# The end of a decoder layer: where the first sums of the last expert, the row statistics and the second token tile's scaling are done

## The reference

```python
hm = x * (1 + sc2) + sh2
# best expert group of 4, the top 2 experts in it, 16 experts in all
for e in range(N_EXPERTS):
    hid = jax.nn.silu(t @ w_gate[e]) * (t @ w_up[e])
    y = y + combine[:, e:e + 1] * (hid @ w_down[e])
x = layer_norm(DEEPNORM_ALPHA * x + g2 * f, ln2_g[l], ln2_b[l])
...
# layer_norm: (x - mean) * rsqrt(var + 1e-5) * g + b, over the 2048 columns of a token
```

## Time and profile before

| what | us |
|---|---|
| median of 3 executions | 1790.05 |
| lowest and highest | 1787.77, 1793.58 |
| the profiled execution | 1788.96 |
| its span from first to last instruction | 1787.1 |
| TensorE busy in it | 1689.7 |
| VectorE busy | 601.3 |
| ScalarE busy | 186.5 |
| last weights landed, from the span's start | 1756.2 |
| last store issued, from the span's start | 1783.4 |

### The profile page before, as it was taken

The page is one execution under the profiler, slowest core; times in us unless marked ns, Lnnn a source line. Parts: engine busy times, 40 slices in busy tenths (PEclk is TensorE's granted clock), DMA queues, the critical chain, the costliest instruction groups (busy, mean ns, idle before and its releaser), DMA issues.

```text
span 1787.1 us, 22339 instructions
## 1 busy us (share of the span) xinstructions
PE 1689.7 (95%) x9444; PEld 992.1 (56%) x9444; DVE 601.3 (34%) x1080; ACT 186.5 (10%) x440; POOL 361.4 (20%) x161
## 2 busy tenths in 40 slices
PE   7799999999999999989899999899999989899986
PEld 6578888888888878643344443333434224334322
DVE  0453657877667143331120311112111111111114
ACT  0001013110011100140100010100101001001001
POOL 0005730277777768200000000000000000000000
PEclk9899999999999999989999999999999999999998
DMA  9997895678877564359958899999999999899995
GB/s 385 423 427 209 352 399 229 277 316 348 341 312 326 244 267 176 123 237 429 424 246 349 361 402 426 426 386 426 424 427 427 427 428 427 367 425 424 428 427 205
DMA packets 51028, 630.10 MB, mean 353 GB/s; under 512 B 5775, under 2 KB 8240, under 8 KB 11848
## 3 DMA queue, kind: packets, MB, share of 16 engines
q1 hardware_dynamic: 49768, 623.15, 84.0%
q10 hardware_dynamic: 1120, 5.01, 0.7%
HBM read 624.47 MB, written 3.67 MB: 351 GB/s over the span
## 4 chain that ended last, share of the span: by engine, by line
PE 74%; DMA 18%; DVE 4%; issue 1%; POOL 1%; SPq 0%; ACT 0%; DVEq 0%; POOLq 0%; ACTq 0%
PE bank L1415 23%; PE bank L865 22%; PE bank L877 10%; PE bank L1177 8%; DMA ring<-in_w_up_gate 7%; DMA ring<-in_ada_w 4%; PE bank L836 3%; DMA region_g<-in_w_up_gate 3%; PE bank L889 3%; PE bank L1253 2%; DMA region_g<-in_w_down 2%; DMA ring<-in_w_down 2%; DVE ada_rows L1944 2%; DMA ring<-in_w_in 1%; POOL ring L736 1%
## 5 line engine op out<-in xcount | busy, mean ns | idle before, releaser
L865 PE MATMUL bank<-ring,region_b 128*64 128x512 f32 x1792 | 407.3, 603 | 33.2 <-DMA ring<-in_w_up_gate 31.3
L736 POOL TENSOR_TENSOR ring<-ring 128x1024 f32<-128x1024 f32 x152 | 359.0, 2389 | 331.5 <-DMA ring<-in_w_in 224.6
L865 PEld LDWEIGHTS bank<-ring,region_b 128*64 128x64 f32 x1792 | 124.5, 138 | 287.6 <-issue 253.3
L877 PE MATMUL bank<-ring,region_f 128*64 128x512 f32 (+1 forms) x1312 | 225.6, 528 | 6.7 <-DMA ring<-in_w_down 6.7
L1415 PE MATMUL bank<-ring,region_a 128*128 128x256 f32 x768 | 171.3, 380 | 0.5 <-ACT region_g L1739 0.5
L1415 PE MATMUL bank<-ring,region_x 128*128 128x256 f32 x768 | 170.4, 379 | 0.9 <-issue 0.7
L1415 PEld LDWEIGHTS bank<-ring,region_a 128*128 128x128 f32 x768 | 145.3, 190 | 23.0 <-issue 2.7
L1415 PEld LDWEIGHTS bank<-ring,region_x 128*128 128x128 f32 x768 | 145.3, 190 | 21.1 <-issue 1.1
L877 PEld LDWEIGHTS bank<-ring,region_f 128*64 128x64 f32 (+1 forms) x1312 | 74.4, 128 | 140.4 <-issue 117.9
L1944 DVE SCALAR_TENSOR_TENSOR bank<-ring,condT,bank 128x512 f32<-128x512 f32 x192 | 144.8, 754 | 5.8
L2378 DVE TENSOR_TENSOR region_a<-bank,region_a 128x512 f32<-128x512 f32 x128 | 79.7, 683 | 179.3 <-PE bank L889 179.0
(11 more groups left out here) (235 smaller groups left out, 1314.6 us busy)
## 6 DMA issues: line engine op xcount, KB each, us to landing
ring<-in_w_up_gate SPq DMA_DIRECT2D x112, 2048.0 KB, 19.3
ring<-in_w_down SPq DMA_DIRECT2D x56, 2048.0 KB, 16.1
ring<-in_ada_w SPq DMA_DIRECT2D x44, 2048.0 KB, 11.9
ring<-in_w_in SPq DMA_DIRECT2D x31, 2048.0 KB, 13.8
region_g<-in_w_up_gate SPq DMA_DIRECT2D x16, 2048.0 KB, 18.3
ring<-in_w_branch SPq DMA_DIRECT2D x8, 2048.0 KB, 14.5
ring<-in_w_out SPq DMA_DIRECT2D x8, 2048.0 KB, 9.9
region_g<-in_w_down SPq DMA_DIRECT2D x8, 2048.0 KB, 23.3
```

What stands on the lines that cost most here:

```text
L736: ins = pool.tensor_tensor(quarter(s, *out)[:, k:k + 4, :], quarter(s, *in0)[:, k:k + 4, :], quarter(s, *in1)[:, k:k + 4, :], op)
L865: last = nc.tensor.matmul(bank_of(x, j)[n * c:n * c + n, 0:2 * m], tokens(x, 8 * half + k), w[:, k % 4, :, m * c:m * c + m], start=(half = ...
L877: last = nc.tensor.matmul(bank_of(x, q)[n * c:n * c + n, 0:m], hidT[x][:, k, :], w[:, k % 4, m * c:m * c + m], start=(k == 0), stop=(k == ...
```

## The change

Four things are altered.

1. For every turn's last expert, `add_up(le, 0)` on TensorE stands ahead of the wait for the last weights, not behind it.
2. For the very last expert VectorE makes four of the eight `bn_stats`, those of columns 0 to 1023 of both tiles, directly behind its sums of output half 0 (`early_stats`), which is ahead of `scale(1)`. The other four, and both `bn_aggr`, follow the sums of output half 1.
3. Tile 1 gets the treatment of tile 0: its own diagonal matrix in `work`, beta by TensorE into the banks 6, 7, 2, 3, and for q = 0, 1, 2 the matmul by TensorE and the copy by ScalarE. Part 3 of tile 1 is centred on VectorE, and then scaled there with beta read from its bank.
4. For both tiles the diagonal matrix is made before the four centred parts, not behind them. SyncE's waits follow: seven stores wait for ScalarE, the last for VectorE.

```diff
--- before.py
+++ after.py
@@ -242,7 +242,8 @@
     return (2 * t + h) % TURN_HALVES % E_PLACES
 
 
-NORM_BANKS = (0, 1, 4, 5)
+NORM_BANKS = ((0, 1, 4, 5), SUM_BANKS)
+BY_PE = ((0, 1, 2, 3), (0, 1, 2))
 LAST_USE = [max(range(i, TURN_HALVES, E_PLACES)) for i in range(E_PLACES)]
 
 
@@ -347,7 +348,7 @@
         hidT = [region_f[:, a:a + 8 * n].rearrange("p (k s) -> p k s", s=n)
                 for a, n in ((0, 64), (512, 32), (768, 32), (1024, 64), (1536, 64))]
         ysb = [sgu_wT[:, 0:512], sgu_wT[:, 512:1024]]
-        row_scale = work[:, 0:P]
+        row_scale = [work[:, 0:P], work[:, P:2 * P]]
         silu_g = [work[:, 0:256], work[:, 256:512]]
         hid = [work2[:, 0:256], work2[:, 256:512]]
         hidx = [None, work[:, 512:640], work[:, 640:768], work[:, 768:1024], work2[:, 512:768]]
@@ -511,6 +512,7 @@
         centred_ready = sem("centred_part_ready")
         scale_ready = sem("diagonal_scale_ready")
         normed_full = sem("normed_part_full")
+        beta_full = sem("beta_of_last_part_full")
 
         block = ctx.enter_context(nc.Block())
 
@@ -717,7 +719,10 @@
             for a in range(TT):
                 for q in range(4):
                     cols = slice(q * 512, (q + 1) * 512)
-                    sp.wait_ge(out_ready if a else tile_out, q + 1)
+                    if q in BY_PE[a]:
+                        sp.wait_ge(tile_out, 4 * a + q + 1)
+                    else:
+                        sp.wait_ge(out_ready, 1)
                     sp.dma_start(out_d[a * P:(a + 1) * P, cols], acc[:, a, cols]).then_inc(s_out, 16)
             sp.wait_ge(s_out, 16 * 4 * TT)
 
@@ -1155,10 +1160,10 @@
             down(0, 1, first).then_inc(half_used, 1)
             if 0 < len(xs) < 3:
                 extra("add F")(1)
-            loaded_half(5, 1)
             early = le == GRP - 1 and not xs
             if early:
                 add_up(le, 0)
+            loaded_half(5, 1)
             down(0, 1, last).then_inc(y_full, 1)
             if len(xs) == 2:
                 extra("add F")(2)
@@ -1568,13 +1573,20 @@
             pe.wait_ge(s_ln2, 32)
             pe.wait_ge(y_ready, 2 * NE + 2)
             pe.wait_ge(t_taken, 3 * NE + 1)
-            for q in range(4):
-                mm(psum[NORM_BANKS[q]][:, :], ident, ln2b[:, q * 512:(q + 1) * 512], True, False)
-            pe.wait_ge(scale_ready, 1)
-            for q in range(4):
-                pe.wait_ge(centred_ready, q + 1)
-                mm(psum[NORM_BANKS[q]][:, :], row_scale, acc[:, 0, q * 512:(q + 1) * 512], False, True)\
-                  .then_inc(normed_full, 1)
+            pe.wait_ge(extras_added, NE)
+            for a in range(TT):
+                for q in range(4):
+                    if a == 1:
+                        pe.wait_ge(m_taken[q], add_job(NE // GRP - 1, GRP - 1, 1, True) + 2)
+                    ins = mm(psum[NORM_BANKS[a][q]][:, :], ident, ln2b[:, q * 512:(q + 1) * 512], True,
+                             q not in BY_PE[a])
+            ins.then_inc(beta_full, 1)
+            for a in range(TT):
+                pe.wait_ge(scale_ready, a + 1)
+                for q in BY_PE[a]:
+                    pe.wait_ge(centred_ready, 4 * a + q + 1)
+                    mm(psum[NORM_BANKS[a][q]][:, :], row_scale[a], acc[:, a, q * 512:(q + 1) * 512], False, True)\
+                      .then_inc(normed_full, 1)
             for g, le, count, here in asked:
                 more_tokens(pe, f"pe{g}_{le}", mybir.EngineType.PE, count, here,
                             lambda xs: expert_pe(pe, mm, g, le, xs))
@@ -1851,10 +1863,11 @@
                     asked.append((g, le, count, here))
             for a in range(TT):
                 root(TT, a)
-            for q in range(4):
-                act.wait_ge(normed_full, q + 1)
-                act.activation(acc[:, 0, q * 512:(q + 1) * 512], psum[NORM_BANKS[q]][:, :], ACT.Copy)\
-                   .then_inc(tile_out, 1)
+            for a in range(TT):
+                for q in BY_PE[a]:
+                    act.wait_ge(normed_full, 4 * a + q + 1)
+                    act.activation(acc[:, a, q * 512:(q + 1) * 512], psum[NORM_BANKS[a][q]][:, :], ACT.Copy)\
+                       .then_inc(tile_out, 1)
             for g, le, count, here in asked:
                 more_tokens(act, f"act{g}_{le}", mybir.EngineType.Activation, count, here,
                             lambda xs: expert_act(act, g, le, xs))
@@ -2393,6 +2406,15 @@
                                 dve.wait_ge(m_full[b], add_job(g, of, q, not more) + 1)
                                 add(psum[SUM_BANKS[b]], q, a, c).then_inc(m_taken[b], 1)
 
+                    def early_stats():
+
+                        if ne == NE - 1:
+                            for b in range(len(SUM_BANKS)):
+                                dve.wait_ge(m_taken[b], add_job(g, le, 0, not more) + 2)
+                            for a in range(TT):
+                                for q in range(2):
+                                    dve.bn_stats(lstat[:, a, q, :], acc[:, a, q * 512:(q + 1) * 512])
+
                     if xs:
                         extra("mark")(xs[0])
                     if xs and le > 0:
@@ -2413,10 +2435,12 @@
                     early = le == GRP - 1 and not xs
                     if early:
                         add_up(le, 0)
+                        early_stats()
                     scale(1)
                     if le == GRP - 1:
                         if not early:
                             add_up(le, 0)
+                            early_stats()
                         add_up(le, 1)
                         for b in range(len(SUM_BANKS)):
                             dve.wait_ge(m_taken[b], add_job(g, le, 1, not more) + 2)
@@ -2451,23 +2475,26 @@
             mark_tokens(0)
             rests = [turn_of_experts(g, g < NE // GRP - 1) for g in range(NE // GRP)]
 
-            dve.wait_ge(s_ln2, 32)
             for a in range(TT):
-                for q in range(4):
+                for q in range(2, 4):
                     ins = dve.bn_stats(lstat[:, a, q, :], acc[:, a, q * 512:(q + 1) * 512])
                 link(ins)
                 dve.bn_aggr(lmv[:, a, :], lstat[:, a, :, :].rearrange("p n s -> p (n s)")).then_inc(l_var, 1)
-                if a == 0:
-                    dve.wait_ge(l_var, TT + 1)
-                    for q in range(4):
-                        part = acc[:, 0, q * 512:(q + 1) * 512]
-                        dve.scalar_tensor_tensor(out=part, in0=part, scalar=lmv[:, 0, 0:1],
-                                                 in1=ln2g[:, q * 512:(q + 1) * 512], op0=ALU.subtract, op1=ALU.mult)\
-                           .then_inc(centred_ready, 1)
-                    dve.wait_ge(l_std, TT + 1)
-                    link(dve.reciprocal(lrstd[:, 0:1], lrstd[:, 0:1]))
-                    dve.tensor_scalar(row_scale, ident, lrstd[:, 0:1], None, ALU.mult).then_inc(scale_ready, 1)
-            scaled(acc, ln2g, ln2b, 1, TT, out_ready)
+            dve.wait_ge(s_ln2, 32)
+            for a in range(TT):
+                dve.wait_ge(l_var, TT + a + 1)
+                dve.wait_ge(l_std, TT + a + 1)
+                link(dve.reciprocal(lrstd[:, a:a + 1], lrstd[:, a:a + 1]))
+                dve.tensor_scalar(row_scale[a], ident, lrstd[:, a:a + 1], None, ALU.mult).then_inc(scale_ready, 1)
+                for q in range(4):
+                    part = acc[:, a, q * 512:(q + 1) * 512]
+                    dve.scalar_tensor_tensor(out=part, in0=part, scalar=lmv[:, a, 0:1], in1=ln2g[:, q * 512:(q + 1) * 512],
+                                             op0=ALU.subtract, op1=ALU.mult).then_inc(centred_ready, 1)
+            dve.wait_ge(beta_full, 1)
+            dve.wait_ge(centred_ready, 4 * TT)
+            last_part = acc[:, 1, 3 * 512:4 * 512]
+            dve.scalar_tensor_tensor(out=last_part, in0=last_part, scalar=lrstd[:, 1:2], in1=psum[NORM_BANKS[1][3]][:, :],
+                                     op0=ALU.mult, op1=ALU.add).then_inc(out_ready, 1)
             for rest in rests:
                 rest()
```

## The result

The changed kernel took 1791.12 us (median of 20 executions, 1786.86 to 1793.22), the kernel before 1787.78 us (20, 1785.26 to 1793.58). The ratio is 1.0017 (95% interval 1.0010 to 1.0023): 3 us slower, still within 0.3%. The forecast was 1784.9 us with a range up to 1788.2, so the time is outside it, on the wrong side of the kernel before.

What follows compares the result with a forecast made beforehand. The kernel's end was taken to be VectorE, then a queue of stores, then one landing. Issuing the eighth store 5.1 us earlier, with the same 3.71 us behind it, turned the median 1790.05 into 1784.9 us, range 1783.0 to 1788.2.

Steps and rivals of the forecast that it cites:

- the zero for everything ahead of the end: Everything before the kernel's end: costed at zero, as the order of TensorE's instructions stays.
- the moved waits of the first three turns: Last experts of the first three turns: moved weight waits costed at zero; up to 1.2 us gain each if weights were late.
- Step 1: Last expert: first sums run at 1755.0 ahead of the weight wait, so the last down half ends 1.2 us earlier.
- Step 2: VectorE at the end: early statistics delay `scale(1)`, leaving it and everything behind 0.50 us earlier, not 1.2; bad bound 0.06.
- Steps 3 and 4: Final tiles: VectorE's part ends at 1776.5; TensorE sets the end, 15 calls unbroken from 1764.0, seventh copy ending 1777.9.
- Step 5: Last stores: eighth issued at 1778.3, 5.1 us earlier, with the same 3.71 us behind it to the span's end at 1782.0.
- my estimate from the Trainium skill: Last store's landing: 2.6 us for 256 KB, which would make the sum about -5.8 us.
- the clock did not fall: Rival, chance 0.20: TensorE idles 1.5 us before the second sums, clock halves, its chain ends 1.7 us later; 1786.6 us.
- the slower rival: Rival, chance 0.04: TensorE at half clock for all 15 calls at the end; median 1797.4 us.
- The faster landing: Rival, chance 0.15: the last store lands in 2.6 us, 0.7 us off the forecast, giving 1784.2 us.
- The stores did queue: Rival, chance 0.12: spaced last stores still block each other at issue, cutting the gain to 3.7 us: 1786.3 us.

Runs made afterwards that it cites:

- with the jump put back: The whole change with 230 never-executed counter instructions added on TensorE, putting the jump back at place 233; 1783.44 us, ratio 0.9971 against the kernel before.
- The run with the split: The change with old code places, tile 1's two early statistics moved behind `scale(1)`; 1782.88 us, ratio 0.9977 against the kernel before.
- the five unchanged ends: Profiled executions of the kernel before, plain and with 20, 26, 46 and 86 never-executed increments; ending on average 35.35 us behind the last down unit's start.

## Why the prediction failed

**The step that failed** is in the first paragraph: "none of that is touched" and "So only the end counts". The order of TensorE's instructions upstream was untouched, as I had read from it, but not their places. By padding alone this is worth 7 us (4 to 9) in the kernel before, more than the whole gain: 4.7 to 4.9 us for one jump of TensorE, and 2.1 to 2.5 us for the half clock behind the wait. The term that failed is the zero for everything ahead of the end. Its stated reason held, for the moved waits of the first three turns cost nothing: with the jump put back the last down unit starts within 0.1 us of where it did. The list of what would be wrong had "an end elsewhere in the kernel than here, such as weights landing at another time than 1756 us", and this is what happened, but with no rival and no price. The price was in the trace: among the jumps of that trace one takes 7.25 us for no wait that the profile names. A rival "the longer program costs one such fetch" would have given up to +7 us behind a gain of 5, hence anything from the forecast to 2 us slower.

**Step 1, the first sums**: right. They begin 3.58 us behind the start and the last down half 1.3 us earlier than before.

**Step 2, the early statistics**: right. They end at 1766.50, `scale(1)` follows at once, and the second sums are 0.68 us earlier where 0.50 was forecast. TensorE's idle time there is 1.42 us, 1.5 in the forecast. The run with the split shows that 0.6 us of this was to be had.

**Steps 3 and 4**: right. VectorE's part never holds TensorE up, the eight beta calls and seven diagonal ones run from 1769.1 to 1782.2, and the copies come 0.86 us apart. That gives the 25.6 us of the forecast.

**Step 5**: the issue of the eighth store was right to 0.1 us, and the term behind it was mis-sized. I kept 3.71 us from issue to the span's end; it was 5.07 us after, 4.65 in the same kernel with its jump put back, and 4.1 to 5.2 in all the others, those with an unchanged end too. The row of 3.71 is the shortest of 14 profiled executions; the other four with this end have 4.2 to 5.0. The stores' line, with the time from issue to landing, in the kernel after:

```profile
L726 SPq DMA_DIRECT2D out<-region_a x8: 332/340/1044, 1777.7 to 1783.6; - x8
...
DMA to landing us min/median/max: 2.5/2.9/4.7
```

The median store does land in 2.9 us, near the 2.6 us of my estimate from the Trainium skill ("DMA: Bandwidth & Descriptors", "Anatomy of one DMA"). The slowest takes 4.7, and the span ends 5.07 us behind the last issue. By that rule the sum would be further from the measurement than by the row.

**The rivals.** At the end the clock did not fall; windows of the kernel after over TensorE's idle stretch, the beta calls and the diagonal ones (width, busy us of PE, PEld, DVE, ACT, POOL, granted clock, DMA share, GB/s):

```profile
1765.73:1767.15 1.42, 0.00 (x1) 0.00 (x0) 1.37 (x3) 0.00 (x0) 0.00 (x0) 1.00 0.00 0
1767.20:1776.00 8.80, 8.80 (x24) 3.79 (x25) 6.93 (x14) 0.59 (x2) 0.00 (x0) 1.00 0.00 0
1776.00:1782.20 6.20, 6.20 (x15) 2.47 (x13) 5.21 (x10) 3.59 (x6) 0.00 (x0) 1.00 0.51 181
```

An idle stretch of 1.42 us was followed by full clock, and with it falls the slower rival too. The fall that did come was upstream, behind the 5.56 us of the jump, where no rival had looked. The faster landing did not come where it counts: the median went from 3.3 us to 2.9, but the longest from 3.9 to 4.7. The stores did queue once: the sixth took 1.04 us to issue where five others took 0.34, which held up the seventh, ready at 1782.85, to 1783.10. That is 0.25 us, and the copy had been ready 0.3 us ahead of the forecast.

**The changed end against its forecast**, with the jump put back: 5.2 us faster by the ratio (3.2 to 7.0), 5.1 forecast. That they agree this closely is in part luck. The medians give 4.2 us, and the end itself is 4.3 us shorter than in the profiled execution before, 3.9 us shorter than the average of the five unchanged ends. The row that the sum started from was out of the common at both of its last terms: its eighth store went at 32.10 us where the other four unchanged ends have 30.4 to 31.1, and its landing of 3.71 us was the shortest. The two errors offset each other in the span.

## What to carry to other kernels

When an edit changes how many instructions an engine's program has, look at every jump to or from code that stands further on: an unrelated jump can move to the start of a fetch block, and then the whole engine waits, and may find its clock at half behind the wait. Sort the branch instructions of the trace by duration before and after, and if one has grown, pad with code that never runs (or move code) before judging the edit. Take the time behind the last store as a range from several executions, not as one row.

## What was not expected of the hardware

- A jump of TensorE to far code, announced ahead, takes 0.31 to 0.47 us; the jump of expert 2, 3 instructions into a block of 256, took 5.06 and 5.27 us, 23 instructions in 2.31, 63 in 0.33, and at places 233 and 253 0.34 to 0.35.
- Each long one of these ended 1.37 to 1.40 us behind the end of a 16 KB packet on the instruction queue q8.
- TensorE's granted clock was 1.00 before the 5.56 and 5.35 us of idleness and 0.50 for 5.1 and 4.3 us behind them; behind 2.60 us it stayed at 1.00.
- A jump that is not announced took 7.2 to 7.9 us for expert 2, the only one that takes it. The other two records of its line, 0.07 us each, are of experts that go on to the section that stands next. An announcement right behind another had no effect on it.
- Of eight stores of 256 KB the slowest landed 4.2 and 4.7 us behind its issue where the median was 2.9. In the changed kernel with its jump put back, the queue is all but empty in the last microseconds, and the span waits for a trickle (windows, columns as above):

```profile
1778.10:1779.50 1.40, 0.00 (x0) 0.00 (x0) 0.00 (x0) 0.00 (x0) 0.00 (x0) 1.00 1.00 363
1779.50:1781.00 1.50, 0.00 (x0) 0.00 (x0) 0.00 (x0) 0.00 (x0) 0.00 (x0) 1.00 0.61 206
1781.00:1782.80 1.80, 0.00 (x0) 0.00 (x0) 0.00 (x0) 0.00 (x0) 0.00 (x0) 0.74 0.04 13
```

The best kernels measured are the change with its jump back at place 233, 1783.44 us, and the same with the statistics split, 1782.88 us; their difference is within what these runs can tell.
